# A two-layer hybrid attention step on one core: one gate set stays in SBUF, narrower score tiles, paired compression products, later waits

## The chip, the cores and the metric

One NeuronCore of a Trainium2 chip runs the whole program. The metric is the device time of one execution in microseconds (us). Three plain runs of the kernel before were timed, and one more was profiled.

## The reference, cut to what matters

The program computes two identical layers (DEPTH = 2) for one prompt of 256 tokens and for 8 sample sequences of one new token each. Each sample sequence has a past of 1024 rows in 8 pages of 128 rows, and a window state of 512 rows. All data is float32. The part that the change is about is this:

```python
# per layer; x is [264, 1024] = 256 prompt tokens + 8 sample tokens
h = rms(x); z = h @ w_in                      # 23 slabs of projections, and 3 mixing gates ma, mb, mc
past = cache_kv[l][page_table]                # 8 sequences x 8 pages x [128, 832]
# compressed keys and values of a sequence: blocks of 32 rows, stride 16 -> 63 blocks
blk = windows(kv, 32, stride=16) + pe
ck, cv = silu(blk @ w1 + b1) @ w2             # hidden 64 each, result 63 x 64 for each of 2 heads
s_sel = nq . sk * scale                       # 64 query rows x 1024 past keys
s_dsa = dq . dk * scale                       # 64 query rows x 1024 past keys
s_win = nq . wk * scale                       # 64 query rows x 512 window keys
# softmax of each, top-k masks, products with the values
gates = sigmoid([ma, mb, mc])
m = sum(gates * einsum('blnc,ncd->blnd', [y_a, y_b, y_c], w_branch))
x = x + m @ w_out
```

## The kernel before, in words

The kernel is written by hand, engine by engine, with semaphores; each engine executes its own list in order, and the lists are the schedule. SP and POOL (GpSimd) issue nearly all DMAs. Activations are kept transposed (features in partitions, 264 tokens in columns). Weights stream through three slots of `slab`; `mix(bank)` computes one of 24 gate blocks (8 for each of the three gates) from such a slab. The 24 mixes are spread over the layer as filler for TensorE, and `take` copies each result out of PSUM into `mix_at[n]`, or takes its sigmoid for the last two. A layer has these stages in this order: projections and gates, prompt attention, prompt compression, the **page stage**, the softmax and value products of the samples, the branch products (line 1394), and the output product (line 1412).

**The page stage** goes over 32 units u = 4s + j, four for each of the 8 sequences s, a unit being a pair of pages. TensorE does for each unit in `for u in range(4, NU)`: four transposes of the page rows (`page_transposes`, line 1239), one quarter of the compression product of the sequence before it (`compress`, line 1281, 8 matmul instructions), at j = 1 the scores of the sequence before it (`page_scores`, line 1269), and at j = 3 the second compression product of sequence s - 2 (`compressed`, lines 1290 and 1292). A float32 matmul of the program appears as two MATMUL instructions in the trace.

`page_scores(s)` uses the array as 32 x 32 tiles. The row quarter r holds a quarter of the keys, the column quarter gives the 32 PSUM partitions of the result. The DSA scores (a = 0) go to column quarter s // 4 with 256 columns. The selected and the window scores (a = 1) go together to column quarter 2 + s // 4 with 256 + 128 = 384 columns. Column quarter 3 - s // 4 is unused.

VectorE does for each unit (`page_taken`): the copy of the transposed rows to `cT` (line 2238, mark C u), then the transposes of the raw keys to `kD` (line 2247, mark D u); at j = 3 also the window keys (line 2258, mark W s) and the addition `join` of the compression halves (line 2283); some small steps of a top-k search are put between them in units 6 to 19. ScalarE does its share of the copies (line 1434), `shift`, `hidden` (the silu, line 1726) and `take_compressed` (line 1434).

`load_keys` issues the page loads of unit u when T u-4 (transposes) and D u-4 are done: two DMAs on SP for the even page (64 and 192 KB, lines 576 and 577), two on POOL for the odd page. There are four slots `kst[:, u % 4]`. SP also issues the window keys and, in the sequences 4 and 5, the halves of the weight slab `m21` (512 KB each).

The first set of eight gate blocks (`raw[0]`) is written to DRAM (`spill[0]`) before the page stage, since the values and keys need its place, and the second set (`raw[1]`) in four parts of 264 KB, issued by POOL within `load_keys` of the sequences 3 to 6 (line 814). Both are read back at the end of the layer (line 725), ahead of the sigmoids (line 1785).

Of the kernel before, what the change touches and what calls it, by code (L numbers as in the profile page):

```python
# [217 lines left out]
def hybrid_step(nc, x_prompt, x_sample, cache_kv, page_table, state_win, state_hgrn, norm_g, w_in,  # L218
# [4 lines left out]
    with ctx:  # L223
# [115 lines left out]
        hid = at(25584, 2, 2, NCS)[0:HD]  # L339
# [3 lines left out]
        o3 = at(28000, 4, 4, NS)  # L343
        PTc = at(28128, ROWS)
        sc4 = at(28192, 64)
        dr = at(28256, 64)
        pn8 = at(28320, 3 * ROWS)[0:NS]
        PTcx = at(28512, NS * (ROWS + NH))[0:NCS]
# [5 lines left out]
        mix_at = [at(5280 + LT * d, LT) for d in range(KD)] + [at(27584 + LT * d, LT) for d in range(KD)]  # L354
        mix_at += [at(30408, LT)] + [at(29088 + LT * d, LT) for d in range(5)] + [at(9000 + LT * d, LT) for d in range(2)]
        raw = (at(5280, KD * LT), at(27584, KD * LT), at(29088, 6 * LT))
        sig = (at(0, KD * LT), at(KD * LT, KD * LT))
        sig_at = [at(LT * n, LT) for n in range(2 * KD)] + mix_at[2 * KD:]
        mT = at(6336, KD, LT)
        mtmp = at(8448, 2, LT)  # L360
        spill = nc.dram_tensor("spill", [2, 128, KD * LT], F32, kind="Internal").ap()
# [20 lines left out]
        class Steps:  # L382
# [15 lines left out]
            def mark(self, step):  # L398
# [7 lines left out]
        S_in, gsel_in, v_in = sem("S_in"), sem("gsel_in"), [sem(f"v_in{i}") for i in range(2)]  # L406
# [21 lines left out]
        y_a = Steps("y_a", ["y 0", "y 1"])  # L428
# [22 lines left out]
        spill_out, back_in = [sem(f"spill_out{a}") for a in range(2)], [sem(f"back_in{a}") for a in range(2)]  # L451
# [13 lines left out]
        pg_v = Steps("pg_v", sum([[f"C {u}", f"D {u}"] for u in range(4)], []) + ["D 4", "W 0", "C 4"] + sum([[f"C {u}", f"D {u}"] + [f"W {u // 4}"] * (u % 4 == 3) for u in range(5, NU)], []))  # L465
        qr_in = sem("qr_in")
        dc_p = Steps("dc_p", sum([[f"w {s - 1}"] * (s > 0) + [f"h {s}"] for s in range(NS - 1)], []) + [f"h {NS - 1}", f"w {NS - 2}"]
                     + ["new", f"w {NS - 1}", "s cmp", "t cmp", "imp", "group imp", "PT", "oT"])
        dc_v = Steps("dc_v", [f"sum {s}" for s in range(NS)] + ["s cmp", "n cmp", "ptx cmp", "imp", "drop", "masked", "new p", "scaled", "ev"])
        dc_a = Steps("dc_a", ["hb 0"] + sum([[f"hid {s}", f"c {s}", f"hb {s + 1}"] for s in range(NS - 2)], []) + [f"hid {NS - 2}", "scores", f"hb {NS - 1}", f"c {NS - 2}", f"hid {NS - 1}", f"c {NS - 1}"]  # L470
# [108 lines left out]
        def load_values(engine, l, s, odd, pages):  # L579

            for k in range(4):
                pg = page_rows(l, pages[s, 2 * k + odd])
                engine.dma_start(V[:, s, 2 * k + odd, :, :], key_and_selected(pg, 128)).then_inc(v_in[odd], 16)  # L583
# [12 lines left out]
        def window_values(engine, l, s):  # L596

            sw = state_win[l, s].rearrange("(t p) c -> p t c", t=4)
            engine.dma_start(Vw[:, s, :, :], sw[:, :, 128:256]).then_inc(v_in[1], 16)
# [15 lines left out]
        def _(sp):  # L615
# [6 lines left out]
            for l in range(DEPTH):  # L622
# [80 lines left out]
                for s in range(2, NS):  # L703
                    load_keys(sp, l, s, 0, pages)
                    if s == 2:
                        sp.wait_ge(spill_out[0], l * 16 + 16)
# [14 lines left out]
                for a in range(2):  # L721

                    sp.wait_ge(spill_out[a], (l + 1) * (16, 64)[a])
                    sp.wait_ge(dx_p.sem, dx_p(l, "x 0"))
                    sp.dma_start(sig[a], spill[a]).then_inc(back_in[a], 16)
# [9 lines left out]
            sp.wait_ge(y_v.sem, y_v(0, "ys"))  # L735
            sp.dma_start(y_sample.rearrange("s o d -> s (o d)"), xsr).then_inc(y_out, 16)
# [3 lines left out]
        def _(pool):  # L740
# [8 lines left out]
            for l in range(DEPTH):  # L749
# [31 lines left out]
                for a in range(2):  # L781
# [12 lines left out]
                    if a == 0:  # L794
                        pool.wait_ge(mx_a.sem, mx_a(l, "m 7"))
                        if l:
                            pool.wait_ge(back_in[0], l * 16)
                        pool.dma_start(spill[0], raw[0]).then_inc(spill_out[0], 16)
# [5 lines left out]
                for s in range(2, NS):  # L804
                    load_keys(pool, l, s, 1, pages)
                    if s == 2:
                        pool.wait_ge(spill_out[0], l * 16 + 16)
                    if s == 3:
# [1654 lines left out]
```

## Time and profile before

| | |
|---|---|
| three plain runs | 1091.92 (median), 1088.34, 1098.45 us |
| the profiled execution: its own time | 1089.36 us |
| its span, first to last instruction | 1087.7 us |
| mean granted TensorE clock | 0.986 |
| TensorE busy | 1045.4 us, 96% |
| VectorE, ScalarE, GpSimd busy | 55%, 39%, 19% |
| bytes moved | 192.83 MB, 177 GB/s mean |

The profile's own time is the span and 1.7 us around it. The page stage lies at about 346 to 424 us in the first layer and at about 879 to 959 us in the second. TensorE's clock has two levels, 2.4 GHz (granted 1.00) and 1.2 GHz (0.50).

### The profile page before, as it was taken

The page shows a single profiled execution, that of the slowest core. Times are in us where ns is not written, and L with a number is a line of the kernel's source. Part 1 is how long each engine was busy: PE and PEld are TensorE (multiplying, and loading weights), DVE is VectorE, ACT ScalarE, POOL GpSimd, SP SyncE. Part 2 cuts the span into 40 slices and gives each one's busy share as a digit, 9 for nine tenths or more (in the row PEclk, how much of TensorE's full clock was granted, in tenths as well). Part 3 has the DMA queues.
Part 4 walks back from the last instruction along what each step waited for, and adds up shares of the span by engine and source line. Part 5 has one row for each costly group of instructions (what it writes and reads, how often), then busy time and mean ns, then how long its engine had stood idle before and what let it go on. Part 6 is the DMA issues. An engine that isn't in the chain of part 4 may idle for free.

```text
span 1087.7 us, 20747 instructions
## 1 busy us (share of the span) xinstructions
PE 1045.4 (96%) x7450; PEld 852.9 (78%) x7450; DVE 595.3 (55%) x1613; ACT 426.8 (39%) x877; POOL 204.4 (19%) x367
## 2 busy tenths in 40 slices
PE   9999999999999999999999999999999999999998
PEld 6888678867777777888888886798777777778886
DVE  4213588877568873224240347887774687631331
ACT  3135433256535774220111554323662566723000
POOL 0300130011124447000030004000203334550000
PEclk9999999999999999999999999999998999999999
DMA  8665358543485899755555544693624869895542
GB/s 230 176 131 160 97 198 245 124 135 110 142 238 176 254 286 266 228 154 151 145 164 141 141 126 117 255 212 112 169 79 144 244 192 283 254 259 206 137 135 78
DMA packets 243108, 192.83 MB, mean 177 GB/s; under 512 B 117950, under 2 KB 224606, under 8 KB 241982
## 3 DMA queue, kind: packets, MB, share of 16 engines
q1 hardware_dynamic: 226368, 140.24, 46.8%
q0 software_dynamic: 15616, 51.19, 14.9%
q8 instruction: 59, 0.97, 0.4%
q14 instruction: 43, 0.35, 0.1%
q10 hardware_dynamic: 1022, 0.07, 0.1%
HBM read 179.03 MB, written 20.80 MB: 184 GB/s over the span
## 4 chain that ended last, share of the span: by engine, by line
PE 80%; DVE 7%; ACT 4%; issue 3%; DVEq 2%; DMA 2%; SPq 2%; ACTq 0%
PE ps L897 21%; PE ps L1034 15%; PE ps L1394 8%; PE ps L1412 5%; PE ps L1269 3%; PE ps L1281 3%; PE ps L1062 2%; PE ps L1239 2%; PE ps L886 2%; PE ps L909 2%; PE ps L1174 1%; PE ps L1162 1%; DMA arena<-in_cache_kv_dram 1%; DVE arena L2238 1%; PE ps L1365 1%
## 5 line engine op out<-in xcount | busy, mean ns | idle before, releaser
L1434 ACT ACTIVATE arena<-ps 64x256 f32<-64x256 f32 (+17 forms) x352 | 186.0, 548 | 259.5 <-PE ps L1404 73.7
L897 PE MATMUL ps<-hT,slab 128*128 128x264 f32 (+1 forms) x1152 | 264.3, 388 | 0.0
L897 PEld LDWEIGHTS ps<-hT,slab 128*128 128x128 f32 (+1 forms) x1152 | 216.8, 190 | 38.5 <-issue 2.5
L1034 PE MATMUL ps<-hT,slab 128*128 128x264 f32 x768 | 186.3, 400 | 0.0
L1034 PEld LDWEIGHTS ps<-hT,slab 128*128 128x128 f32 x768 | 148.4, 197 | 31.8 <-DVEq L2152 3.2
L565 POOL DMA_DIRECT2D arena<-in_cache_kv_dram x64 | 34.6, 541 | 347.1 <-PE ps L975 200.3
L1394 PE MATMUL ps<-Y,slab 128*128 128x264 f32 x384 | 85.8, 386 | 0.0
L1394 PEld LDWEIGHTS ps<-Y,slab 128*128 128x128 f32 x384 | 73.0, 190 | 12.5
L1281 PE MATMUL ps<-arena,w 128*128 128x128 f32 x512 | 70.3, 282 | 5.3 <-ACT arena L1434 3.5
L1882 DVE SCALAR_TENSOR_TENSOR arena<-arena,gains 128x264 f32<-128x264 f32 x26 | 11.0, 488 | 114.8 <-ACT arena L1517 114.8
L2238 DVE COPY arena<-ps 64x256 f32<-64x256 f32 x96 | 59.4, 619 | 23.8 <-PE ps L1239 22.7
L1281 PEld LDWEIGHTS ps<-arena,w 128*128 128x128 f32 x512 | 62.6, 194 | 10.1 <-DVE arena L2247 5.1
L1412 PE MATMUL ps<-arena,slab 128*128 128x264 f32 x256 | 58.4, 387 | 2.3 <-DVEq L2408 2.3
L1412 PEld LDWEIGHTS ps<-arena,slab 128*128 128x128 f32 x256 | 48.0, 190 | 11.0 <-DVEq L2408 3.1
L1593 ACT ACTIVATE arena<-ps 128x264 f32<-128x264 f32 x48 | 18.7, 390 | 95.7 <-PE ps L1034 95.4
L576 POOL DMA_DIRECT2D arena<-in_cache_kv_dram x64 | 34.4, 538 | 93.1 <-DVE arena L2247 29.0
L583 POOL DMA_DIRECT2D arena<-in_cache_kv_dram x64 | 45.1, 709 | 31.8 <-PE ps L1281 16.2
L2247 DVE STREAM_TRANSPOSE arena<-arena 128x256 f32<-128x256 f32 x128 | 48.1, 412 | 3.1 <-PE ps L1239 2.1
L1239 PE MATMUL ps<-cst,arena 128*128 128x128 f32 x256 | 40.6, 286 | 7.2 <-DMA arena<-in_cache_kv_dram 3.5
L1640 ACT ACTIVATE arena<-arena,st 128x128 f32<-128x128 f32 (+1 forms) x96 | 42.3, 443 | 8.0 <-DVEq L2152 7.0
L1269 PE MATMUL ps<-arena,slab 32*32 32x384 f32 (+1 forms) x1024 | 45.0, 432 | 0.5 <-DVE arena L2258 0.5
L1239 PEld LDWEIGHTS ps<-cst,arena 128*128 128x128 f32 x256 | 29.9, 146 | 19.2 <-issue 11.6
(387 smaller groups left out, 1436.7 us busy)
## 6 DMA issues: line engine op xcount, KB each, us to landing
slab<-in_w_in_dram SPq DMA_DIRECT2D x46, 1024.0 KB, 5.7
slab<-in_w_in_dram SPq DMA_DIRECT2D x80, 256.0 KB, 4.1
arena<-in_cache_kv_dram POOLq DMA_DIRECT2D x64, 192.0 KB, 4.0
arena<-in_cache_kv_dram SPq DMA_DIRECT2D x64, 192.0 KB, 4.1
arena<-in_cache_kv_dram POOLq DMA_DIRECT2D x64, 128.0 KB, 6.5
arena<-in_cache_kv_dram SPq DMA_DIRECT2D x64, 128.0 KB, 6.8
slab<-in_w_branch_dram SPq DMA_DIRECT2D x16, 512.0 KB, 5.8
slab<-in_w_out_dram SPq DMA_DIRECT2D x8, 1024.0 KB, 4.7
```

The lines of the kernel that those rows point to most:

```text
L583: engine.dma_start(V[:, s, 2 * k + odd, :, :], key_and_selected(pg, 128)).then_inc(v_in[odd], 16)
L897: last = mm(ps[0:job[3], n % 2, 0:LT], v[:, k, job[2]:job[2] + job[3]], hT[:, k, :], start=(k == 0), stop=(k == KD - 1))
L1034: last = mm(ps[:, bank, 0:LT], v[:, k, (d % 2) * 128:(d % 2) * 128 + 128], hT[:, k, :], start=(k == 0), stop=(k == KD - 1))
L1239: last = nc.tensor.transpose(ps[:, 4 + u % 2, o:o + 128], kst[:, j, i, c:c + 128], ident)
L1269: last = mm(out, queries_of(r, c, a, s), block_keys(s, a)[quarter[r], :, 32 * c:32 * c + 32], start=s % 4 == 0 and c == 0, stop=s % 4 == 3 ...
L1281: last = mm(ps[:, 6 + s % 2, kv * 128:(kv + 1) * 128], w1[:, kv, t, :], cT[:, s % 2, kv, t, :], start=(t == 0), stop=(t == ST - 1))
L1394: last = mm(ps[:, d % 4, 0:LT], v[:, j, dd * 128:dd * 128 + 128], Y[:, a, j, :], start=(j == 0), stop=(j == 3))
L1412: last = mm(ps[:, d % 4, 0:LT], v[:, k, (d % 2) * 128:(d % 2) * 128 + 128], mT[:, k, :], start=(k == 0), stop=(k == KD - 1))
L1434: return A(out, in_, ACT.Copy, scale=scale)
L1640: A(x[:, j, :], x[:, j, :], ACT.Exp, scale=-1.0, bias=st[:, c + j:c + j + 1], accum_out=sa[:, c + j:c + j + 1])
L2238: last = TC(blocks_of(s, j, u)[:, :, 0], pairs_of(4 + w % 2, 0, u))
L2247: last = nc.vector.transpose(block_keys(s, a)[:, 2 * j:2 * j + 2, :], kst[:, j, :, c:c + 128])
```

## The change: what it does

1. **Second gate set in SBUF.** The arena is laid out anew: the second set lies at its end, the temporary PTcx and gate blocks 17 to 21 lie in `w1` (whose weights are used up by then). `spill[1]`, its four writes on POOL with their waits, its read back, and the waits of ScalarE and VectorE for it are gone. The sigmoids of the second set work in place, those of the third are two instructions instead of one.
2. **Scores.** The selected scores (256 columns) stay in column quarter 2 + s // 4, and the window scores (128 columns) go to column quarter 3 - s // 4. For each c and r there are three matmuls instead of two. ScalarE copies the result out in three pieces instead of two.
3. **Paired compression products.** The second product is made for two sequences at once: `hid` holds both with 127 columns, `compressed(p)` runs at j = 3 of odd sequences only, and `take_compressed(p)` copies the keys of both sequences in one instruction and the values in two. The last pair comes after mix 17, and the one of sequence 6 ahead of the scores' masks is gone.
4. **VectorE's order in units 5 to 31.** At j = 2 only C u is done; at j = 3 the order is C u, D u-1, D u.
5. **Single waits.** Values are awaited by halves (sequences 0 to 3, then 4 to 7). The output product waits for gate step b 2 6, and for b 2 7 only ahead of its last part k = 7. At the start, the transpose of small parameters comes after four of the eight x transposes. At the end, the sample rows are copied out of PSUM by VectorE and ScalarE, half each.

The core of the diff:

```diff
-                            for a in range(2):
-                                out = ps[quarter[2 * a + s // 4], r, 0:(NPG + 4 * a) * 32].rearrange("p (n j) -> p n j", j=32)
-                                last = mm(out, queries_of(r, c, a, s), block_keys(s, a)[quarter[r], :, 32 * c:32 * c + 32],
+                            for a, q, n in ((0, s // 4, slice(0, NPG)), (1, 2 + s // 4, slice(0, NPG)), (1, 3 - s // 4, slice(NPG, NPG + 4))):
+                                out = ps[quarter[q], r, n.start * 32:n.stop * 32].rearrange("p (n j) -> p n j", j=32)
+                                last = mm(out, queries_of(r, c, a, s), block_keys(s, a)[quarter[r], n, 32 * c:32 * c + 32],
...
                     if part == 0:
                         taken_from(4 * s + 3)
                         if s >= 2:
-                            pe.wait_ge(dc_a.sem, dc_a(l, f"c {s - 2}"))
+                            pe.wait_ge(dc_a.sem, dc_a(l, f"c {s // 2 - 1}" if s % 2 else f"hid {s - 2}"))
...
-                def compressed(s):
-                    pe.wait_ge(dc_a.sem, dc_a(l, f"hid {s}"))
-                    b = 6 + s % 2
+                def compressed(p):
+                    pe.wait_ge(dc_a.sem, dc_a(l, f"hid {2 * p + 1}"))
+                    n = 2 * NCS + 1
                     for x in range(2):
-                        mm(ps[:, b, 256:256 + NCS], w2[:, x, :], hid[:, 0, x, :], start=(x == 0), stop=(x == 1))
+                        mm(ps[:, 7, 256:256 + n], w2[:, x, :], hid[:, 0, x, 0:n], start=(x == 0), stop=(x == 1))
...
-                    if j == 3 and s >= 2:
-                        compressed(s - 2)
+                    if j == 3 and s >= 3 and s % 2:
+                        compressed(s // 2 - 1)
...
-                compressed(NS - 2)
...
-                pe.wait_ge(v_in[0], (l + 1) * NS * 4 * 16)
-                pe.wait_ge(v_in[1], (l + 1) * NS * 5 * 16)
                 for k in range(2):
+                    pe.wait_ge(v_in[k][0], (l + 1) * 4 * 4 * 16)
+                    pe.wait_ge(v_in[k][1], (l + 1) * 4 * 5 * 16)
...
-                pe.wait_ge(ga_v.sem, ga_v(l, "b 2 7"))
+                pe.wait_ge(ga_v.sem, ga_v(l, "b 2 6"))
...
                     for k in range(KD):
+                        if d == 0 and k == KD - 1:
+                            pe.wait_ge(ga_v.sem, ga_v(l, "b 2 7"))
...
-                    if s == 3:
-                        pool.wait_ge(mx_a.sem, mx_a(l, "m 15"))
-                        if l:
-                            pool.wait_ge(back_in[1], l * 16)
-                    if 3 <= s < 7:
-                        c = slice((s - 3) * KD * LT // 4, (s - 2) * KD * LT // 4)
-                        pool.dma_start(spill[1, :, c], raw[1][:, c]).then_inc(spill_out[1], 16)
...
-                    page_taken(w)
+                    page_copied(w)
+                    if j == 3:
+                        keys_taken(w - 1)
+                    if j != 2:
+                        keys_taken(w)
...
-                    TC(xsr.rearrange("p (b c) -> p b c", b=2), ps[0:NS, 0:2, :]).then_inc(y_v.sem, y_v.mark("ys"))
+                    TC(xsr[:, 0:512], ps[0:NS, 0, :]).then_inc(y_v.sem, y_v.mark("ys"))
```

## Rows read from the trace of the kernel before

**Rows 1.** The page: the chain that ended last, shares of the span.

```profile
PE 80%; DVE 7%; ACT 4%; issue 3%; DVEq 2%; DMA 2%; SPq 2%; ACTq 0%
```

**Rows 2.** Stretches of the page stage: length, busy PE, PEld, DVE, ACT, POOL, clock, DMA, GB/s.

```profile
346.00:356.00 10.00, 8.59 (x115) 7.08 (x114) 8.73 (x19) 6.69 (x12) 3.72 (x7) 1.00 0.59 158
...
386.00:397.00 11.00, 10.43 (x129) 8.58 (x128) 8.38 (x18) 8.57 (x17) 4.97 (x10) 1.00 0.95 293
...
911.00:922.00 11.00, 8.70 (x73) 7.24 (x60) 8.45 (x19) 6.58 (x14) 4.35 (x9) 0.84 1.01 326
```

**Rows 3.** Timeline: first and last of eight scores, one sequence between (idle before in brackets).

```profile
346.59 2.81 PE L1269 MATMUL ps<-arena,slab 32*32 32x256 f32 x64 [0.23 <-DVE arena L2258]
...
400.67 0.66 PE L1239 MATMUL ps<-cst,arena 128*128 128x128 f32 x4
...
401.36 5.33 ACT L1434 ACTIVATE arena<-ps 64x256 f32<-64x256 f32 x10 [1.62 <-PE ps L1239]
401.36 1.44 DVE L2238 COPY arena<-ps 64x256 f32<-64x256 f32 x2 [2.40 <-PE ps L1239]
...
402.83 0.77 DVE L2247 STREAM_TRANSPOSE arena<-arena 128x256 f32<-128x256 f32 x2
...
403.53 0.55 DVE L2238 COPY arena<-ps 64x256 f32<-64x256 f32 x1
...
404.91 0.54 POOL L577 DMA_DIRECT2D arena<-in_cache_kv_dram  x1
...
417.00 2.81 PE L1269 MATMUL ps<-arena,slab 32*32 32x256 f32 x64
```

**Rows 4.** Line 1269 by form, 366.5 to 369.6 us: one sequence's scores.

```profile
L1269 PE MATMUL ps<-arena,slab 32*32 32x384 f32 x32 | 2.8, 484 | 0.0
L1269 PE MATMUL ps<-arena,slab 32*32 32x256 f32 x32 | 2.2, 380 | 0.0
```

**Rows 5.** Line 1269 alone in the first 60 ns of a sequence's scores: PE, PEld.

```profile
366.58:366.64 0.06, 0.05 (x8) 0.05 (x12) 1.00 0.58 205
```

**Rows 6.** PE's groups over the span: busy us, mean ns, idle before.

```profile
L1394 PE MATMUL ps<-Y,slab 128*128 128x264 f32 x384 | 85.8, 386 | 0.0
L1281 PE MATMUL ps<-arena,w 128*128 128x128 f32 x512 | 70.3, 282 | 5.3 <-ACT arena L1434 3.5 <-DVE arena L2258 1.7
...
L1365 PE MATMUL ps<-arena 128*8 128x128 f32 x512 | 14.8, 273 | 0.0
...
L1290 PE MATMUL ps<-arena,w 64*128 64x63 f32 x64 | 10.5, 284 | 2.1 <-ACT arena L1726 2.1
...
L1292 PE MATMUL ps<-w,arena 64*63 64x64 f32 x64 | 7.0, 230 | 0.0
```

**Rows 7.** Waits of DVE and ACT in 346 to 424 us: total, times, longest.

```profile
DVE arena L2238 <- PE ps L1239: 10.3, 7, 2.4
...
ACT arena L1434 <- DVE arena L2238: 6.6, 9, 1.6
```

**Rows 8.** Waits of PE for pages: 878 to 960 us, then 346 to 424 us.

```profile
PE ps L1239 <- DMA arena<-in_cache_kv_dram: 2.1, 1, 2.1
...
PE ps L1239 <- DMA arena<-in_cache_kv_dram: 1.3, 1, 1.3
```

**Rows 9.** DMA issues, median us to landing: whole span, then 376 to 386 us.

```profile
arena<-in_cache_kv_dram POOLq DMA_DIRECT2D x64, 192.0 KB, 4.0
...
arena<-in_cache_kv_dram POOLq DMA_DIRECT2D x4, 192.0 KB, 5.8
```

**Rows 10.** Timeline: the start, the stage behind the scores, the output product, the end.

```profile
21.57 7.39 PE L886 MATMUL ps<-arena,slab 128*128 128x264 f32 x32 [0.26 <-DMA slab<-in_w_in_dram]
...
428.57 0.65 PE L1290 MATMUL ps<-arena,w 64*128 64x63 f32 x4 [1.05 <-ACT arena L1726]
...
516.89 3.38 PE L1412 MATMUL ps<-arena,slab 128*128 128x264 f32 x14 [1.14 <-DVEq L2408]
...
1083.47 1.21 DVE L2426 COPY arena<-ps 8x1024 f32<-8x1024 f32 x1 [0.18 <-PE ps L1422]
```

More of the change, by code:

```diff
@@ L405, in hybrid_step @@
         w1_in, rest_in = sem("w1_in"), sem("rest_in")
-        S_in, gsel_in, v_in = sem("S_in"), sem("gsel_in"), [sem(f"v_in{i}") for i in range(2)]
+        S_in, gsel_in, v_in = sem("S_in"), sem("gsel_in"), [[sem(f"v_in{k}{i}") for i in range(2)] for k in range(2)]
         slab_in = [sem(f"slab_in{i}") for i in range(NSLOT)]
@@ L450, in hybrid_step @@
         mx_a = Steps("mx_a", [f"m {n}" for n in range(NMIX)])
-        spill_out, back_in = [sem(f"spill_out{a}") for a in range(2)], [sem(f"back_in{a}") for a in range(2)]
+        spill_out, back_in = sem("spill_out"), sem("back_in")
         at_p = Steps("at_p", ["s 00", "s 01"] + sum([[f"t {a}{t}{g}" for t, g in GH] + sum([[f"s {a + 1}{t}"] * (a < 2) + [f"o {a}{t}"]
@@ L582, in load_values @@
                 pg = page_rows(l, pages[s, 2 * k + odd])
-                engine.dma_start(V[:, s, 2 * k + odd, :, :], key_and_selected(pg, 128)).then_inc(v_in[odd], 16)
+                engine.dma_start(V[:, s, 2 * k + odd, :, :], key_and_selected(pg, 128)).then_inc(v_in[s // 4][odd], 16)
         def first_keys(engine, l, odd, pages):
@@ L1725, in hidden, with take_compressed @@
                     for kv in range(2):
-                        last = A(hid[:, kv], hsd[:, 2 * kv:2 * kv + 2, :], ACT.Silu, bias=hbias[0:HD, kv:kv + 1])
+                        last = A(hid[:, kv, :, (NCS + 1) * (s % 2):(NCS + 1) * (s % 2) + NCS], hsd[:, 2 * kv:2 * kv + 2, :], ACT.Silu, bias=hbias[0:HD, kv:kv + 1])
                     last.then_inc(dc_a.sem, dc_a.mark(f"hid {s}"))
-                def take_compressed(s):
-                    act.wait_ge(dc_p.sem, dc_p(l, f"w {s}"))
-                    copy(ckd[:, s, :], ps[:, 6 + s % 2, 256:256 + NCS])
-                    copy(CV[0:NCS, s, :], ps[0:NCS, 6 + s % 2, 320:448]).then_inc(dc_a.sem, dc_a.mark(f"c {s}"))
+                def take_compressed(p):
+                    act.wait_ge(dc_p.sem, dc_p(l, f"w {p}"))
+                    copy(ckd[:, 2 * p:2 * p + 2, :], ps[:, 7, 256:384].rearrange("p (s n) -> p s n", s=2)[:, :, 0:NCS])
+                    for i, h in enumerate(halves):
+                        last = copy(CV[0:NCS, 2 * p + i, :], ps[h.start:h.start + NCS, 7, 384:512])
+                    last.then_inc(dc_a.sem, dc_a.mark(f"c {p}"))
                 for w in range(4, NU):
@@ L1739, in _ @@
                         hidden(s - 2)
-                    if s >= 2 and j == 3:
-                        take_compressed(s - 2)
+                    if s >= 3 and s % 2 and j == 3:
+                        take_compressed(s // 2 - 1)
                     if s and j == 3:
@@ L1779, in _ @@
                 for a in range(3):
-                    if a < 2:
-                        act.wait_ge(back_in[a], l * 16 + 16)
-                        x = sig[a]
-                    else:
-                        x = raw[2]
-                    A(x, x, ACT.Sigmoid).then_inc(ga_a.sem, ga_a.mark(f"sg {a}"))
+                    if a == 0:
+                        act.wait_ge(back_in, l * 16 + 16)
+                    for x in sig[a]:
+                        last = A(x, x, ACT.Sigmoid)
+                    last.then_inc(ga_a.sem, ga_a.mark(f"sg {a}"))
                 take(3, ACT.Sigmoid)
@@ L1790, in _ @@
                 copy(xr[:, 0, t * 512:t * 512 + 512], ps[:, 4 + t, :]).then_inc(y_a.sem, y_a.mark(f"y {t}"))
+            act.wait_ge(y_p.sem, y_p(0, "ys"))
+            copy(xsr[:, 512:1024], ps[0:NS, 1, :]).then_inc(y_a.sem, y_a.mark("ys"))
         @block.vector
```

85 lines of the change are left out of this document (43 added, 42 removed).

## The prediction

> **What bounds the kernel now.** I read the page first: TensorE is busy for 96% of the span and is 80% of the chain that ended last [rows 1]. So time goes only where TensorE's own work on the chain gets shorter, or where it stands idle. Then I read the page stage in stretches of some 10 us, since most of the change lies there. The eight scores of the first layer start from 346.59 to 417.00 us [rows 3], so a sequence takes 70.4 / 7 = 10.06 us. TensorE is busy for 79 to 95% of a stretch, VectorE for 76 to 87%, and in the stretches with the weight halves the DMA engines for 95% or more, at 293 and 326 GB/s [rows 2]. The reader should see that four resources are near each other: a faster TensorE runs soon into the others. The timeline of one sequence shows the coupling [rows 3]: scores 2.8 us, then the transposes of unit j = 2, and only then can VectorE go on; it had stood idle for 2.40 us, ScalarE for 1.62. In the whole stage of the first layer VectorE loses 10.3 us in 7 such waits, 1.5 us each [rows 7]. That idle time is the room which shorter scores can use.
>
> **Scores.** In one sequence the two forms run at the same time [rows 4]: 32 instructions of 384 columns span 2.8 us and 32 of 256 columns lie within that. On one 32 x 32 tile eight instructions follow each other (four c, two for each float32 matmul), and four row quarters run side by side. 384 columns at 2 cycles and 2.4 GHz are 0.32 us, eight are 2.56 us, and with a start and end of 0.2 us that gives the 2.8 us. The longest tile afterwards has 256 columns: 8 x 0.213 = 1.71 us, with the same 0.2 about 1.9 us. The gain is 0.86 us for a sequence, 13.8 us for 16. This holds if 96 instructions can be started in 1.9 us, one per 20 ns. Two rows bound that: eight matmuls started in 60 ns, under 8 ns each [rows 5], and the densest long group, line 1365, goes at 14.8 / 512 = 29 ns [rows 6]. The latter has four column tiles of 128 columns each, and 107 / 4 = 27 ns is what its columns need anyway, so it is not an issue limit by itself. I take the first; by the second 96 x 29 ns = 2.8 us and the gain is nothing.
>
> The Trainium skill ("TensorE: Matmul & The Clock Gate", section Back-to-back issue gap) gives an issue floor of about 25 ns for each matmul; as an estimate by that page, 96 would take 2.4 us and the gain would be 0.4 us for a sequence instead of 0.86, some 7 us less in all. The first rows of a sequence's scores [rows 5] speak against such a floor between different tiles, for a burst of eight.
>
> **Compression products.** Lines 1290 and 1292 are busy for 10.5 + 7.0 us [rows 6], 1.1 us a sequence, of which about 0.95 lies on the chain (the next instruction overlaps their end). A pair now costs four instructions of 127 columns, priced by line 1281 (70.3 / 512 = 0.137 us, 128 columns), and four of 64 columns at 7.0 / 64 = 0.11: 0.99 us in place of 1.9. At most 0.9 x 8 = 7 us go. ScalarE does three copies for a pair instead of four, but puts all three in one unit, where TensorE waits for them (mark c) before the next sequence's first quarter. Ten of its copies, each of 64 x 256, take 5.33 us [rows 3], so one is 0.53 us at most; a smaller one more in that unit costs odd sequences under 0.53 us, and even ones, with two fewer, gain more. I count nothing for it.
>
> **Page stage, what comes late next.** With both, TensorE needs 10.06 - 0.86 - 0.45 = 8.75 us for a sequence, less what it now stands idle. Three others: VectorE has 8.73 us of work in the first 10 us (top-k steps included) and 8.38 in 11 us later, and ScalarE 6.69 and 8.57 [rows 2], at most 7.8 for a sequence. The third is the loop of a page slot: in the sequence of [rows 3] the transposes of j = 2 start at 400.67, VectorE ends D at 403.60, and POOL issues the odd page's second DMA at 404.91; it lands 4.0 us later as the median of the span, and 5.8 in the full stretch [rows 9], so at 408.9, or 410.7. The next transposes of this slot come a period later, at 410.7: a margin of 1.8 us at the usual latency, none at 5.8. The new order on VectorE puts C of j = 3 (0.55 us) ahead of that D [rows 3], so the load goes about 0.45 us later. The loop then takes 4.24 + 0.45 + 4.0 = 8.7 us at the least, and 9.1 to 9.3 if latency is 0.5 us above the median, since more bytes move per us. For the reordering itself there is a gain: ScalarE waited 6.6 us in 9 times for VectorE's C [rows 7], which now comes 0.77 us earlier at j = 3, and compress waits for both (5.3 us idle at line 1281 [rows 6]). So I expect 9.3 us for a sequence in place of 10.06, a gain of 0.75 us each (above the loop's 9.1 to 9.2 by a little, for VectorE's 8.73 us in the early sequences), where TensorE alone would allow 1.3. 14 periods give **10.5 us**. Bounds: 0 (the page loop or issue limits as described in the rivals) and 14 x 1.3 = 18 us.
>
> **The end of the page stage.** The last scores and the last product of sequence 6 stand on the chain with no other engine beside them: 0.86 + 0.95 us. It is given back in part behind mix 17: the last pair is wider, and ScalarE copies three pieces where TensorE already waited 1.05 us for the silu and then for the copies [rows 10]; 0.5 us. Net 1.3 us, **2.6 us** for both layers; bounds 1 and 4.
>
> **Second gate set.** 1.06 MB less are written in the page stage and read back later. The return trip costs nothing now: line 1394 runs with no idle time at all [rows 6]. The writes lie among the page loads of sequences 3 to 6; the one long stall for pages is in that stretch in both layers, 1.3 and 2.1 us [rows 8], and around the second TensorE's granted clock was 0.84 in the mean of 11 us [rows 2], so at its lower level for part of them, 1.8 us of work lost. The weight halves stay. 0.27 MB at 326 GB/s [rows 2] are 0.83 us of DMA time in each of four sequences, so I count 0.5 us a layer beside the loop above, **1 us**; bounds 0 and 5 (both stalls and the low clock gone).
>
> **Output product.** TensorE stands idle for 1.14 us until VectorE has added the last gate block [rows 10], in both layers. A block is eight instructions at line 1394, 8 x 85.8 / 384 = 1.8 us [rows 6], so the one before the last is added by then, and seven of eight parts, 14 instructions that take 3.38 us [rows 10], cover the rest. 2.3 us for two layers less some start of the pipeline: **2.0 us**. Bounds 1.5 and 2.3.
>
> **Start and end.** The x transposes may begin 0.9 us earlier, but the second slab's arrival holds TensorE at 21.57 us [rows 10] in either order: 0. The last copy takes 1.21 us [rows 10] and is split: **0.4 us**. Values by halves: the wait did not hold TensorE before, 0, unless the values become late. The waits for the spill on ScalarE and VectorE were long met: 0. The third sigmoid in two instructions lies under line 1394: 0.
>
> **Sum.** 10.5 + 2.6 + 1.0 + 2.0 + 0.4 = 16.5 us; 1089.4 - 16.5 = 1072.9 us against the profiled execution. The median of the three runs is 2.6 us above it, the fastest 1.0 below. I say 1074, with a part of that offset.
>
> **Rivals.**
> - *TensorE alone decides* (0.12): the page loads come quicker without the spill, and the full 1.3 us of each period go. 18 + 3 + 3 + 2 + 0.5 = 26 us, 1063 to 1065. For it: the usual latency of 4.0 us leaves the loop at 8.7 us. Against it: VectorE's 8.7 us in the early stretches.
> - *The matmul issue decides* (0.16): 96 instructions take as long as 64 did, or 2.4 us. Then 0 to 7 us come from the scores, 3 from the pairs (they make room that the loop doesn't fill), 4 elsewhere: 7 to 11 us, 1079 to 1084. For it: no row shows more than a burst at under 20 ns.
> - *The pages decide, on the faster side* (0.12): DMA engines at 95 to 100% in the stretches with weight halves [rows 2] hold two or three sequences at 10 us, and latency grows to 5 us elsewhere, so that a period is 9.7: 5 + 5.5 = 10 to 11 us, about 1079 to 1081.
> - *The late slot, slower than before* (0.04): the load of j = 2 goes 0.45 us later and the page latency rises to 6.6 us (5.8 in the full stretch [rows 9] and 0.8 for a longer queue), in all sequences and not in one. The loop is then 4.7 + 6.6 = 11.3 us, over 14 periods 17 us more than now, less the 6 us elsewhere: 1100 us. It decides from a latency of 10.06 - 4.7 = 5.4 us on.
> - *More low clock* (within the others' ranges): TensorE has more short idle spots. The fall in [rows 2] cost 1.8 us; two more would take 3.6 us of the gain.
>
> **Chances and range.** The forecast, 1069 to 1078 us, has 0.56; the rivals have the rest as given. What a measurement of this kernel can tell from no change is about 1%, 11 us, so faster means under about 1081: forecast, the first rival, and most of the second and third, 0.83. Within 1%: 0.13. Slower: 0.04. The range of 1064 to 1084 leaves out the slower rival and the tails of the others.
>
> **What the changed profile would show.** Line 1269: 1536 instructions, about 1.9 us for a sequence, three forms side by side. VectorE's idle time ahead of C at j = 2 falls from 1.5 us to some 0.7. Scores start every 9.3 us. TensorE's waits for pages become more and shorter, in place of two long ones. Lines 1290 and 1292 have half the instructions. The idle time at line 1412 is under 0.2 us. Wrong would be: scores still at 2.4 us or more (issue), periods of 8.5 us (TensorE alone), or page waits in each sequence and periods of 10 us.

## The result and the profile after

The changed kernel takes 1084.9 us in the median of 20 runs, the kernel before 1089.1 us in the median of its 20. The ratio is 0.9949, 95% interval 0.9931 to 0.9967: faster by 0.5%. By the ratio that is some 5.5 us (the two medians are 4.2 us apart), where 15 were forecast. The profiled execution has a span of 1080.9 us (before: 1087.7).

The page's line for TensorE, and its waits for pages by line 1236 (line 1239 before), first in 340 to 425 us, then in 875 to 960 us; columns: total, times, longest.

```profile
PE 1027.2 (95%) x7898; PEld 846.0 (78%) x7898; DVE 593.5 (55%) x1613; ACT 427.5 (40%) x874; POOL 200.1 (19%) x359
```

```profile
PE ps L1236 <- DMA arena<-in_cache_kv_dram: 4.6, 4, 2.6
PE ps L1236 <- issue: 3.3, 6, 0.8
...
PE ps L1236 <- issue: 5.8, 7, 1.5
PE ps L1236 <- DMA arena<-in_cache_kv_dram: 4.1, 2, 2.8
```

TensorE's busy time fell by 18.2 us, from 1045.4 to 1027.2, but the span by 6.8. So nearly two thirds of the saved work came back as idle time. The rows say where: it waits for pages for 4.6 and 4.1 us by name, where it waited 1.3 and 2.1 [rows 8], and "issue" at the same line adds 3.3 and 5.8, where it added 0.6 and 1.4. Together that is 17.8 us against 5.4.

The page stage of the first layer as one window, from the first scores to the eighth (columns: length, busy PE, PEld, DVE, ACT, POOL, clock, DMA share, GB/s), the kernel before and then the changed one:

```profile
346.60:417.00 70.40, 65.42 (x824) 53.23 (x825) 55.10 (x129) 52.73 (x101) 34.67 (x61) 1.00 0.87 261
```

```profile
344.90:417.50 72.60, 61.02 (x1026) 53.15 (x1027) 55.25 (x129) 52.59 (x98) 32.59 (x57) 0.98 0.80 239
```

TensorE needs 4.4 us less and the stage is 2.2 us longer; the DMA engines move less per us than before. So TensorE's own work doesn't set the end, nor does the mean rate of the bytes. In a full stretch, though, the DMA engines are busy for 97% at 296 GB/s, and the longest wait of the layer lies there (same columns; a part of the time at the lower clock):

```profile
385.00:397.00 12.00, 8.96 (x128) 7.94 (x115) 7.93 (x19) 6.67 (x14) 4.29 (x8) 0.90 0.97 296
```

In the second layer the stage went from 73.1 to 70.9 us: both layers together take 143.5 us, as before. The whole gain of the page stage is gone, in a change whose scores and compression products are there to shorten it.

The scores themselves, one sequence by form, and the first 90 ns of it (PE, PEld):

```profile
L1266 PE MATMUL ps<-arena,slab 32*32 32x256 f32 x64 | 2.2, 380 | 0.0
L1266 PE MATMUL ps<-arena,slab 32*32 32x128 f32 x32 | 2.1, 278 | 0.0
```

```profile
407.26:407.35 0.09, 0.08 (x12) 0.08 (x21) 1.00 0.99 387
```

Three column quarters run side by side, and twelve matmuls start within 90 ns. The sequence takes 2.2 us where 1.9 were forecast and 2.8 were taken before [rows 4]. That first burst isn't the pace of the whole: the 96 instructions start over 1.9 us, one in 20 ns in the mean.

What happened within one sequence, the timeline around the longest wait (idle before in brackets):

```profile
386.29 0.35 SPq L580 DMA_DIRECT2D arena<-in_cache_kv_dram  x1
...
387.33 1.19 DVE L2236 COPY arena<-ps 64x256 f32<-64x256 f32 x2 [0.47 <-PE ps L1236]
...
388.62 0.66 PE L1236 MATMUL ps<-cst,arena 128*128 128x128 f32 x4 [0.44 <-DMA arena<-in_cache_kv_dram]
...
389.32 0.73 DVE L2236 COPY arena<-ps 64x256 f32<-64x256 f32 x1 [0.80 <-PE ps L1236]
...
389.86 1.43 DVE L2245 STREAM_TRANSPOSE arena<-arena 128x256 f32<-128x256 f32 x4
...
390.83 0.33 SPq L580 DMA_DIRECT2D arena<-in_cache_kv_dram  x1
...
394.00 0.69 PE L1236 MATMUL ps<-cst,arena 128*128 128x128 f32 x4 [2.60 <-DMA arena<-in_cache_kv_dram]
394.49 1.91 PE L1278 MATMUL ps<-arena,w 128*128 128x128 f32 x8
```

VectorE has finished C of unit j = 2 at 388.52. In the order of before it would now transpose that unit's keys and free the slot. In the new order it stands idle for 0.80 us, for C of j = 3 comes first, and that waits for TensorE's transposes, which wait for their own page (0.44 us). Then all four key transposes go together and the loads of two slots leave in one burst, from 390.83 on.

The longest wait, 2.60 us up to 394.00, is for another slot, the one of j = 0. Its loads were issued from 386.29 to 387.10, before the put-off transposes and their burst, and behind a window load (issued at 385.08) and half of the weight slab (at 385.55). SP's 192 KB of it took 7.1 us to land. The clock fell then too (0.90 in the mean of 385 to 397 us), and the next compression quarter takes 1.91 us for 1.06. In all profiles in which the lower clock lies within a page stage, TensorE had just stood idle, or still did, for 1.2 to 2.8 us in one piece, though not each long wait brought a fall.

So the waits are best counted by slot. This table adds up the idle time ahead of TensorE's page transposes, both layers, from the timelines (us); it has runs 1 and 2 of the experiments too.

| slot of unit | before | new order alone (run 2) | old order in the changed kernel (run 1) | changed |
|---|---|---|---|---|
| j = 0 | 4.0 | 7.1 | 5.5 | 10.4 |
| j = 1 | 0 | 0 | 0 | 0.9 |
| j = 2 | 0 | 0.4 | 0.2 | 3.3 |
| j = 3 | 1.4 | 2.2 | 4.7 | 3.1 |
| sum | 5.4 | 9.6 | 10.3 | 17.8 |

TensorE's busy time in the two stages fell by 13.0 us, and these waits grew by 12.4. Most of them stand at the slot of j = 0, where both long waits of before stood as well, and not at the slot whose reload the new order puts off. Run 12, with the page stage of before, has 5.0 us, all at j = 0, which tells how far two profiles of one code agree.

Three places outside the page stage gained: the start of the first weight product, the output product, and the last copy.

```profile
11.74 5.16 PE L883 MATMUL ps<-arena,slab 128*128 128x264 f32 x22
...
512.81 5.50 PE L1410 MATMUL ps<-arena,slab 128*128 128x264 f32 x24
...
1076.72 0.68 DVE L2427 COPY arena<-ps 8x512 f32<-8x512 f32 x1 [0.18 <-PE ps L1420]
```

Line 1410 has no idle time ahead of it any more (1.14 us before [rows 10]). From the eighth scores of the first layer to the first scores of the second it is now 456.2 us, where the profile before has 462.4. Half of that isn't the change's: in the profile before the lower clock lies over 13.7 us of this stretch, in the changed one over 6.8, which is 3.4 us of TensorE's work. Of the 2.8 us left, 1.1 are the output product. The rest lies around the end of the page stage: the scores of the compressed keys (line 1328 before, 1324 now) start 11.9 us behind the eighth scores, where they started 13.1 us behind them, which is 1.1 us with none of the lower clock in between.

### The profile page after: what moved, and what is told of

Same layout as the page of the kernel before. It is cut to its first block, busy times and chain, and to the rows that moved or that the text cites. A ratio compares the mean times of both kernels' runs of the same rounds, so it can differ in the third digit from the quotient of the medians.

```text
span 1080.9 us, 21628 instructions
## 1 busy us (share of the span) xinstructions
PE 1027.2 (95%) x7898; PEld 846.0 (78%) x7898; DVE 593.5 (55%) x1613; ACT 427.5 (40%) x874; POOL 200.1 (19%) x359
## 4 chain that ended last, share of the span: by engine, by line
PE 77%; DVE 7%; issue 4%; ACT 4%; DMA 3%; DVEq 3%; SPq 2%; ACTq 0%
PE ps L894 21%; PE ps L1031 15%; PE ps L1390 8%; PE ps L1410 5%; PE ps L1278 3%; PE ps L1266 2%; PE ps L1059 2%; DMA arena<-in_cache_kv_dram 2%; PE ps L1236 2%; PE ps L883 2%; ACT arena L1432 2%; PE ps L1171 1%; PE ps L1159 1%; PE ps L1361 1%; DVE top L1929 1%
## 5 line engine op out<-in xcount | busy, mean ns | idle before, releaser
L1432 ACT ACTIVATE arena<-ps 64x256 f32<-64x256 f32 (+18 forms) x347 | 187.2, 558 | 255.6 <-PE ps L1400 72.3
L1432 ACT ACTIVATE Y<-ps 128x264 f32<-128x264 f32 x24 | 9.4, 391 | 85.9 <-PE ps L894 85.9
L1591 ACT ACTIVATE arena<-ps 128x264 f32<-128x264 f32 x38 | 14.8, 390 | 60.2 <-PE ps L1031 59.9
```

Source lines behind the costliest of these rows:

```text
L1432: return A(out, in_, ACT.Copy, scale=scale)
```

## The experiments

All ratios are to the kernel before on the same chip. "Page stage" is the time from the first scores to the eighth, both layers added up, in one profile; before 143.5, changed 143.5. Run 12, whose page stage has the code of before, has 143.1. Where the lower clock lies within a stage it lengthens it too, and this is said beside the numbers. Sums of the waits for pages take in the idle time that the profile calls "issue" at the same line; in run 9 both are gone together.

**1. VectorE's old order** in the changed kernel.

```diff
                     s, j = w // 4, w % 4
-                    page_copied(w)
-                    if j == 3:
-                        keys_taken(w - 1)
-                    if j != 2:
-                        keys_taken(w)
+                    page_taken(w)
```

> The changed kernel with VectorE's order of the kernel before: at j = 2 the keys are transposed right behind their copy. Theory A (the deferred key transposes delay the loads of slot 2, tie them to the arrival of the unit behind, and send two slots' loads in one burst): faster than the changed kernel, by 4 to 9 us, so a ratio to the kernel before of 0.986 to 0.991; scores every 9.3 to 9.6 us; 192 KB page loads land in about 4.0 us again in the first three sequences (4.4 to 4.7 us in the changed kernel); waits for pages under 3 us a layer. Theory B (the bytes per us decide: a faster TensorE only asks for the pages earlier): no change against the changed kernel within 2 us, ratio 0.993 to 0.997, and the waits for pages stay at 4 us a layer and more. Theory C (the new order helped, since ScalarE's copies and the compression product come earlier): slower than the changed kernel by 2 to 5 us, ratio about 1.0.

Measured: 0.9904 (0.987 to 0.9938), 1078.8 us; page stage 138.1 us. This is Theory A's gain, some 5 us over the changed kernel, though the two intervals just overlap. Its waits for pages add up to 5.4 us in the first layer, more than the 3 us expected, and 4.6 in the second. In 340 to 426 us:

```profile
PE ps L1236 <- issue: 4.3, 5, 1.2
...
PE ps L1236 <- DMA arena<-in_cache_kv_dram: 1.1, 1, 1.1
```

The 192 KB loads of POOL issued in 346 to 376 us land in 4.3 us (4.7 changed, 3.8 before). But run 12, with the order and loads of before, has 4.5 in that stretch, so these differences are no larger than those between profiles of one code. Of the 5.4 us of the stage, 1.7 are the lower clock, which lies over 3.4 us of the changed kernel's stages and over none of this run's. So the order is a part of the cause, and not all of it.

**2. The new order alone** in the kernel before (the same edit, the other way round).

> The kernel before with VectorE's new order alone. Theory A: slower than before by 2 to 6 us (1.002 to 1.006), with page waits of 3 us a layer or more and longer landings of the 192 KB loads. Theory B: within 1 us of before, for TensorE is still the slowest. Theory C: faster by 1 to 3 us, since ScalarE's waits for VectorE's copies (6.6 us in the first layer) become shorter.

Measured: 1.0040 (1.001 to 1.007), slower. Page stage 150.0 us, 6.5 more. Waits for pages in the first layer, and the loads of 346 to 376 us (KB each, median us to landing):

```profile
PE ps L1239 <- DMA arena<-in_cache_kv_dram: 4.4, 3, 2.8
```

```profile
arena<-in_cache_kv_dram POOLq DMA_DIRECT2D x12, 192.0 KB, 5.1
```

The order costs 4 us even where TensorE is the slowest. Theories B and C fall for this part. Of the 6.5 us, 4.2 are waits for pages (9.6 against 5.4), and nearly all of those 4.2 stand at the slots of j = 0 and 3, not at the one that is put off. Up to 3.4 more are the lower clock, over 10.2 us of these stages against 3.4. The landing is 5.1 us here and 3.8 and 4.5 in the profiles of before and run 12, which have the old order, and in the second layer 4.6 against 4.1, 4.0 and 5.3 in three of them (before, run 12, run 3); that the burst makes the loads slower is possible, but not shown.

**3. The score tiles alone** in the kernel before: the three-way loop over (a, q, n) in `page_scores`, and the three copies out.

> The kernel before with the score tiles alone (three matmuls for two, three copies out). The scores take 2.2 us in place of 2.8. Theory A: most of 16 x 0.6 = 9.7 us shows, 6 to 10 us, ratio 0.991 to 0.994, as the slots are reloaded in the old order. Theory B: the page loads take it back, 0 to 3 us, ratio 0.997 to 1.0, with waits for pages of over 5 us a layer.

Measured: 1.0009 (0.9978 to 1.0039); page stage 144.6 us. Against Theory A as I had put it: 16 x 0.6 us of TensorE's time went, and nothing came out, with the old order of VectorE. A part of this is the clock: it is lower over 10.2 us of this run's stages and over 3.4 before, which is 3.4 us of TensorE's work, so that at the same clock the stage would be 2.3 us shorter. The timed executions had a mean granted clock of 0.984, those of the kernel before beside them 0.988. The waits for pages are 7.4 us against 5.4. It fits Theory B's number. But B's reason, the bytes per us, isn't shown by this, and runs 5 to 8 speak on it.

**4. The writes of the second gate set kept** in the changed kernel.

```diff
+                    if s == 3:
+                        pool.wait_ge(mx_a.sem, mx_a(l, "m 15"))
+                    if 3 <= s < 7:
+                        c = slice((s - 3) * KD * LT // 4, (s - 2) * KD * LT // 4)
+                        pool.dma_start(copy_of_set[:, c], at(RAW1, KD * LT)[:, c]).then_inc(set_out, 16)
```

> The changed kernel with the four writes of 264 KB of the second gate set kept on POOL at their old places; nobody reads them back or waits for them. Theory A says that the bytes are not what decides: 0 to 2 us slower than the changed kernel. Theory B, the bytes decide: 1.06 MB a layer at 285 to 326 GB/s are 3.3 to 3.7 us, so 5 to 7 us slower than the changed kernel, ratio to the kernel before 1.000 to 1.002.

Measured: 0.9967 (0.9938 to 0.9995); page stage 143.4 us. The difference from the changed kernel, 2 us, is within the intervals, and the page stage is the same. Theory A's number; the 1.000 to 1.002 of Theory B lie outside the interval. 0.26 MB in each of four sequences don't show.

**5. The weight slab m21 behind the page loads**, on top of run 1: `send("m21")` after the loop over s.

> The changed kernel with VectorE's old order, and with the two halves of the weight slab m21 (1 MB a layer) sent behind the last page loads and not within sequences 4 and 5. Theory B (bytes per us in the full stretches): the three periods around the halves shrink by 0.5 to 1 us each, 3 to 6 us in all, ratio to the kernel before of 0.985 to 0.988. Theory A (the round trip of a slot: transposes, VectorE, issue, landing): under 2 us, ratio 0.989 to 0.992.

Measured: 0.9874 (0.9839 to 0.9909), page stage 134.7 us (138.1 in run 1). By the profile 3.4 us, by the ratios 3 us, with overlapping intervals: between the two theories. The bytes of 1 MB beside the page loads count for some of it.

**6. Half the rows of each page**, on top of run 1. From sequence 2 on only rows 0 to 63 are loaded, so these sequences' keys and values of compression are partly those of an earlier one; the number of loads, waits and instructions is the same.

> The changed kernel with VectorE's old order, and page loads of sequences 2 to 7 that bring only the first 64 of the 128 rows of each page (the other rows keep the data of an earlier sequence), with the same number of loads and waits. Theory B: pages no longer hold anyone; periods of 8.7 to 9.0 us from sequence 2 on, 12 to 16 us faster than the same kernel with whole pages, ratio 0.976 to 0.980. Theory A in its strict form (issue and fixed latency decide): landings stay at 3.5 to 4 us, periods of 9.5 us, under 5 us faster, ratio 0.986 to 0.990.

Measured: 0.9863 (0.9829 to 0.9896); page stage 130.1 us, 8 us less than in run 1. The stage in the first layer:

```profile
343.90:409.00 65.10, 57.98 (x1024) 51.35 (x1024) 54.44 (x129) 51.65 (x98) 32.02 (x57) 1.00 0.65 171
```

With half the bytes (171 GB/s) the periods are 9.1 to 9.9 us in the first five and 8.7 to 9.0 in the last two. TensorE's own work is 58.0 / 7 = 8.3 us a sequence, but the waits for pages are down to 1.4 us in this layer and the stage still takes 65 us. What TensorE waits for now is ScalarE (3.5 us in 340 to 420 us, not counting the silu behind the stage) and VectorE (2.3 us). So about 65 us a layer is what these two, busy for 51.7 and 54.4 us, leave in this order of the lists; no run takes work from them, so that is argued. The ratio is in Theory A's range, but the loads land in 2.6 to 3.2 us and not in 3.5 to 4, so fewer bytes do land sooner; the 12 to 16 us of Theory B didn't come.

**7. Each page load divided by its user**, on top of run 1, with all bytes.

```diff
-            for k in range(4):
+            for part, k in ((0, 0), (0, 1), (1, 0), (1, 1), (0, 2), (0, 3), (1, 2), (1, 3)):
...
-                if s:
-                    engine.wait_ge(pg_p.sem, pg_p(l, f"T {u - 4}"))
-                    engine.wait_ge(pg_v.sem, pg_v(l, f"D {u - 4}"))
-                engine.dma_start(kst[:, u % 4, odd, 0:128], pg[:, 0:128]).then_inc(page_in[u % 4][odd], 16)
-                engine.dma_start(kst[:, u % 4, odd, 128:512], pg[:, 320:704]).then_inc(page_in[u % 4][odd], 16)
+                if part == 0:
+                    if s:
+                        engine.wait_ge(pg_p.sem, pg_p(l, f"T {u - 4}"))
+                    engine.dma_start(kst[:, u % 4, odd, 128:384], pg[:, 320:576]).then_inc(page_in[u % 4][odd], 16)
+                else:
+                    if s:
+                        engine.wait_ge(pg_v.sem, pg_v(l, f"D {u - 4}"))
+                    dst = kst[:, u % 4, odd, :].rearrange("p (g c) -> p g c", g=4)[:, 0:4:3, :]
+                    engine.dma_start(dst, key_and_selected(pg, 0)).then_inc(key_in[u % 4][odd], 16)
```

Part 0 is what TensorE alone reads, part 1 the keys, which VectorE alone reads; VectorE waits for `key_in`.

> The changed kernel with VectorE's old order, and with each page load divided by who uses it and not by columns: 128 KB for the compression (columns 320 to 575), issued when TensorE has transposed the slot, some 2 to 3 us earlier than now, and 128 KB of keys (columns 0 to 127 and 576 to 703), issued when VectorE has transposed them. TensorE waits for the first alone, VectorE for the second. Same bytes, same number of loads. Theory A: TensorE's waits for pages fall under 2 us a layer; periods of 9.2 to 9.5 us, 5 to 9 us faster than with the old loads, ratio 0.982 to 0.986. Theory B: the bytes are the same, so the waits go over to VectorE and the ratio stays at 0.989 to 0.992.

Measured: 0.9836 (0.9811 to 0.9861), 1071.9 us; page stage 132.5 us. The same bytes in the same number of loads, and 5.5 us of the stage are gone; it is within 2.4 us of the stage with half the bytes. The wait for pages in the first layer:

```profile
PE ps L1241 <- DMA arena<-in_cache_kv_dram: 0.5, 1, 0.5
```

Theory A is shown, as far as the 138.1 us of run 1 go: what held TensorE was the round trip of a slot through VectorE, not how many bytes the DMA engines could move. TensorE also waits for fewer bytes of each page now, 128 KB instead of 256, but its load doesn't land sooner for that: POOL's and SP's together take 4.2 and 5.5 us in the median of the stage's two halves in the first layer, where the 192 KB loads of run 1 took 4.2 and 4.7. So it is the earlier issue that counts.

**8. The divided loads with the new order**, that is, the changed kernel with its own order of VectorE.

> The changed kernel as it is, with VectorE's new order, and the divided loads of the run before. Theory A: what the new order cost came by way of the slot that TensorE waits for; with its own load tied to TensorE alone, the new order costs nothing more: within 2 us of the divided loads with the old order, ratio 0.982 to 0.987. If the new order costs in another way (the burst of four slots' loads, the late window keys), it stays 3 us or more slower than the old order.

Measured: 0.9857 (0.9827 to 0.9888), page stage 131.8 us; its first layer:

```profile
342.50:408.10 65.60, 58.64 (x1024) 51.35 (x1024) 54.26 (x129) 51.93 (x98) 37.13 (x58) 1.00 0.91 264
```

The order that cost 4 us alone and 5 us in the changed kernel costs nothing measurable once TensorE's pages no longer wait for it. And 264 GB/s go through with 0.4 us of waits for pages in the first layer (1.4 in the second), at landings of 5.2 to 5.4 us: here neither more bytes per us nor a longer landing did harm, as the load was issued early enough.

**9. The divided loads alone** in the kernel before.

> The kernel before with the divided page loads alone. Theory A (page slots hold TensorE only once it is faster): before, TensorE waited 3.4 us for pages and 2.0 us in unnamed waits of the same line, so 2 to 5 us faster, ratio 0.995 to 0.998, periods of 9.8 us. If the loop held the kernel before as much as the changed one, 8 us and more, 0.992 or less.

Measured: 0.9991 (0.9968 to 1.0014); page stage 138.9 us, 4.6 less than before. TensorE has no wait for pages left in either layer. The stage says what was expected, the whole says less, and the interval allows 3.5 us of it. The timed executions had a mean granted clock of 0.987, those of the kernel before beside them 0.989; among the latter 0.01 of clock goes with some 11 us. As an estimate from that, 2 us of the missing gain are the clock.

**10. The divided loads and the score tiles** in the kernel before.

> The kernel before with the divided page loads and the score tiles. Theory A: against the divided loads alone the scores now show what they did not show by themselves, 6 to 9 us of 16 x 0.6 = 9.7 us; ratio to the kernel before 0.987 to 0.991, periods of 9.2 to 9.4 us. Rival: something else than the page slots takes the scores' gain back (VectorE or ScalarE), then 0 to 3 us against the divided loads alone, ratio 0.994 or more.

Measured: 0.9942 (0.9916 to 0.9969); page stage 132.6 us. This closes the square for the scores:

| page stage, us | old loads | divided loads |
|---|---|---|
| scores as before | 143.5 | 138.9 |
| narrower score tiles | 144.6 | 132.6 |

With the old loads the tiles give -1.1 us, with the divided loads 6.3 us of TensorE's 9.7, and 0.5% of the time. The lower clock lies over 3.4 us of the upper left stages, 10.2 of the lower left and none of the right ones; with half of that taken off the left column reads 141.8 and 139.5, and the tiles give 2.3 us there. The stage is as expected, but the ratio is above the 0.987 to 0.991 of Theory A, at the edge of the rival's. What holds back the rest of the 9.7 us isn't shown; the rival names VectorE and ScalarE.

**11. All three together**: old order, divided loads, m21 behind.

> The changed kernel with VectorE's old order, the divided page loads, and the weight slab m21 behind the page loads: the three that helped together. Waits for pages are nearly gone with the divided loads alone (0.5 us in the first layer), so m21 gives under 2 us more: ratio 0.981 to 0.985. If the bytes still stretch sequences 4 and 5, 3 to 4 us more, 0.980.

Measured: 0.9856 (0.9825 to 0.9888), 1072.2 us; page stage 131.5 us. No better than the divided loads alone, and the ratio is just above both ranges of the expectation. m21 gave 3 us in run 5 and 1 us of the stage here, so there, too, it was the late slot that made the bytes count. Runs 7, 8 and 11 can't be told apart; all three beat both kernels, run 7 with the lowest ratio.

**12. The single waits alone** (edit 5) in the kernel before.

> The kernel before with edit 5 alone: values awaited by halves, the output product's later wait, the small transposes after four of the eight x transposes, and the last copy by two engines. From the profiles, the idle time ahead of the output product goes (1.14 us twice), the last copy ends 0.5 us earlier, and the first product of a weight slab starts 1.7 us earlier; the page stage stays at about 143 us in both layers together. If all three reach the end, 4.5 us, ratio 0.996; by the prediction's own step (nothing from the start) 2.4 us, ratio 0.998.

Measured: 0.9974 (0.9942 to 1.0007); page stage 143.1 us. Between the two expectations, which the interval doesn't separate. Its first weight product starts 1.0 us earlier than the 13.48 us of before, while the changed kernel's starts 1.7 us earlier, at 11.74:

```profile
12.48 5.16 PE L888 MATMUL ps<-arena,slab 128*128 128x264 f32 x22
```

Between the first weight product and the page stage nothing changed: the profile before needs 318.2 us from 28.4 to 346.6, the changed one 318.2 from 26.7 to 344.9. So the 1.7 us of the start reach the page stage undiminished.

## Why the prediction was right or wrong

The prediction was wrong: the time was 1 us above the range of 1064 to 1084, and the gain a third of the forecast.

- **The step that failed is "Page stage, what comes late next", 10.5 us.** It was 0: 143.5 us before and after. The prediction followed the loop of one slot, the one of j = 2, with a landing near the median, and found it just short enough for periods of 9.3 us. The runs show that waits for pages took back nearly all that TensorE had saved there, 12.4 of 13.0 us, and that only 3.3 of their 17.8 us stand at j = 2; 10.4 stand at j = 0, where a load can take 7.1 us in the full stretch and where the two long waits of [rows 8] had stood before. That slot's loop wasn't in the sum. The third rival named the side, the full stretches with the weight halves, but kept half of the gain.
- **The deferral in the same step** was set at 0.45 us, about the length of one copy. It is up to 1.3 us, since the copy put first waits for TensorE's transposes of j = 3, and those for their own page: a late page delays the reload of another slot. I counted the reordering as a gain for ScalarE; runs 1 and 2 show it as a cost of 5 and 4 us, a part of it at the lower clock. How it lengthens the waits at j = 0, where nothing is put off, is open. The landing was set at 4.5 us and was 4.7 in the first 30 us of the stage, so that term was about right in the median; it is the long ones that were missing.
- Had the order stayed, the step would still have been too high: run 1 gives 138.1 us, 5.4 less in place of 10.5, and run 3 shows nothing from the scores by themselves. My 9.3 us for a period was near the 9.3 of run 6 (65.1 us for 7 periods), but that is luck: it came from the loop at j = 2, and in run 6 hardly a page is in the way.
- **Scores, 0.86 us a sequence:** right in kind, 0.6 in size. The term of 0.2 us for start and end is 0.5 with 96 instructions: in the scores at 407.26 us the twelve tiles start within 73 ns, but the last instructions of the 256-column tiles start from 1.55 to 1.83 us behind the first. Four of these eight tiles start their third instruction one turn, 0.2 us, later than the others, and why is open. The issue rival fell in the sizes it named, 2.4 and 2.8 us; a limit of 20 ns in the mean isn't excluded. The Trainium skill ("TensorE: Matmul & The Clock Gate", section Back-to-back issue gap) gives an issue floor of about 25 ns for a small matmul; as an estimate by it, 96 would take 2.4 us. This trace doesn't agree between different tiles: twelve start within 90 ns, and all 96 take 2.2 us.
- **Compression products:** 5.7 + 4.4 us busy in place of 10.5 + 7.0 [rows 6], 7.4 us gone where 7 were counted.
- **End of the page stage, 1.3 us a layer:** 1.1 in the first layer, by the start of the compressed keys' scores. In the second the profile has a gap of 1.76 us ahead of the last compression quarter, for which it names no releaser and at which the kernel has no wait, and more of the lower clock, so that from the eighth scores to the end it is 136.4 us for 135.3. The same gap (1.7 to 2.0 us, 0.9 in run 6) stands in runs 1, 4 and 5, and not with the divided loads nor in the kernel before; its cause is open.
- **Second gate set, 1 us:** run 4 shows 2 us, uncertain, and none of it in the page stage. It can't be told from 0. That the long wait and the fall of the clock in [rows 2] and [rows 8] come from these writes isn't borne out: both are there in the first layer of the changed kernel, which has no such writes (2.6 us, and a clock of 0.90 in 385 to 397 us).
- **Output product, 2.0 us:** right; the idle time went from 1.14 us to nothing, twice. **The last copy, 0.4 us:** 0.5.
- **Start, 0:** wrong, 1.7 us. I read the wait at 21.57 us as the time of a slab that comes whenever it comes. But in the changed kernel it came 1.7 us sooner with the rest; run 12 has 1.0 us of that at the first product, with the same order of the transposes.
- The slower rival didn't happen as a whole. Its late issue at j = 2 did, but the 0.4 us of waits at that slot in run 2 aren't what made that run slower.

What stays open: why the divided loads alone (run 9) shorten the stage by 4.6 us and the time by 1, as far as the lower clock of those executions doesn't explain it (in the profile the first scores start 2.6 us later than before, with 13.7 us of the lower clock ahead of them for 6.8); how the start's 1.7 us divide between the transposes' order and the slab's earlier arrival; and how the order of VectorE reaches the slot of j = 0.

## What to carry to other kernels

Where a buffer is read by two engines and reloaded when both are done, its round trip is set by the later of the two, and a faster first engine only waits longer: count the loop (use, second use, issue, landing) of every slot, with the longest landing of the full stretches and not the median alone, before counting what the faster engine saves, and reload each part when its own reader is done. When an instruction is put ahead of one that frees a buffer, ask what the first one waits for: if that is itself a load, one late page delays the next. And try an edit that gives nothing once more after the wait that hid it is gone; the score tiles showed nothing in the time before it and 0.5% after.

## What the hardware showed that I had not expected

The landing of a 192 KB load varies between profiles of the same code as much as between the orders: in the first 30 us of the first page stage it is 3.8 us in the kernel before and 4.5 in run 12, which has the same page stage, and 4.7 in the changed kernel. A longer landing need not cost anything: 264 GB/s with 0.4 us of waits for pages in run 8, at landings of 5.2 to 5.4 us, against 239 GB/s with 7.9 us of waits in the changed kernel. The lower clock lies over very different parts of the same code from profile to profile. Over the whole span it is 29.7 us in the profile before and 24.2 in the changed one, so that some 2.8 of the 6.8 us by which the two profiled spans differ are the clock's.
